# Two transformer blocks in one kernel: first product by blocks of rows, an expert's whole matrix per transfer, attention probabilities scaled after the values

## What is computed

```python
h = rmsnorm(x, attn_norm);  proj = h @ w_in                         # block 1, start
# mixture of experts, per group of 8 experts
hid = silu(einsum('td,edf->tef', h, w_gate[g])) * einsum('td,edf->tef', h, w_up[g]) * combine
y = y + einsum('tef,efd->td', hid, w_down[g])
# block 2, kind 0: window of 128 keys to either side, all context keys, and a sink column
s_loc = where(band_mask, q_a @ k_a.T * scale, -inf);  s_ctx = q_a @ k_ac.T * scale
p = softmax(concat([s_loc, s_ctx, sink]));  o_a = p_loc @ v_a + p_ctx @ v_ac
# block 2, kind 1: neighbourhood of 16 columns, bias rpb, and all context keys
p = softmax(concat([q_b @ k_b.T * scale + bias (masked), q_b @ k_bc.T * scale]))
o_b = p_loc @ v_b + p_ctx @ v_bc
x_new = x + g1 * concat([rms_norm(o_a), rms_norm(o_b)]) @ w_out
```

## Time and profile before

| | us |
|---|---|
| median of three runs | 819.42 |
| lowest, highest | 817.73, 819.96 |
| the profiled execution's own time | 819.99 |
| its span, first to last instruction | 818.2 |
| TensorE busy | 752.5 (92%) |
| mean granted clock of TensorE | 0.986 |

### The profile page before, as it was taken

One profiled execution on the slowest core, in us unless ns is written; L12 is line 12 of the kernel. 1 busy time (PEld: TensorE's weight loads), 2 busy tenths in 40 slices (PEclk: granted clock), 3 DMA queues, 4 the chain that ended last, 5 costly groups with the idle time before them and its releaser, 6 DMA issues. The chain is left out here.

```text
span 818.2 us, 14415 instructions
## 1 busy us (share of the span) xinstructions
PE 752.5 (92%) x5881; PEld 551.5 (67%) x5881; DVE 453.9 (55%) x820; ACT 321.0 (39%) x563; POOL 39.4 (5%) x31
## 2 busy tenths in 40 slices
PE   8999999899998998767868899898999999999998
PEld 5978976554745754543635687656547888888886
DVE  3899755544542233022130796589667766577665
ACT  4667333410442233031240854566542533434431
POOL 1000021010000000000000033100010000000000
PEclk9999999999999999999899999999999999999999
DMA  8894459979899999999999995500008354565201
GB/s 282 288 355 158 152 211 397 333 271 347 327 402 400 407 403 408 402 404 409 403 404 403 401 264 201 205 2 2 1 1 287 137 194 154 185 228 205 103 1 51
DMA packets 130501, 208.40 MB, mean 255 GB/s; under 512 B 7909, under 2 KB 55302, under 8 KB 130318
## 3 DMA queue, kind: packets, MB, share of 16 engines
q1 hardware_dynamic: 129518, 205.39, 68.9%
q10 hardware_dynamic: 864, 2.18, 0.8%
q0 software_dynamic: 64, 0.05, 0.0%
HBM read 206.51 MB, written 1.08 MB: 254 GB/s over the span
## 5 line engine op out<-in xcount | busy, mean ns | idle before, releaser
L2608 DVE TENSOR_TENSOR unit_parts<-ring,unit_parts 128x2048 fp32r<-128x2048 f32 x33 | 75.5, 2289 | 57.2 <-ACT unit_parts L1936 57.2
L1936 ACT ACTIVATE unit_parts<-ring 128x2048 fp32r<-128x2048 f32 x33 | 62.9, 1912 | 73.9 <-PE psa L1313 43.0
L1312 PE MATMUL psv<-column_parts,unit_parts 128*128 128x512 f32 (+1 forms) x192 | 65.5, 389 | 1.6 <-DVE arena L2686 1.4
L1312 PE MATMUL psa<-column_parts,unit_parts 128*128 128x512 f32 (+1 forms) x192 | 65.1, 388 | 0.0
L1020 PE MATMUL psv<-ring,arena 128*32 128x256 f32 x976 | 54.5, 380 | 0.2 <-DMA ring<-in_w_up_dram 0.2
L1313 PE MATMUL psv<-column_parts,unit_parts 128*128 128x256 f32 (+1 forms) x192 | 52.0, 271 | 0.0
L1313 PE MATMUL psa<-column_parts,unit_parts 128*128 128x256 f32 (+1 forms) x192 | 52.0, 271 | 0.0
L2729 POOL TENSOR_TENSOR small<-small,consts 128x2 f32<-128x2 f32 (+4 forms) x15 | 28.2, 1883 | 472.7 <-DVE small L2460 246.2
L954 PE MATMUL psa<-arena 128*128 128x128 f32 x224 | 34.2, 325 | 14.4 <-DMA arena<-in_w_in_dram 14.2
L1020 PEld LDWEIGHTS psv<-ring,arena 128*32 128x32 f32 x976 | 30.8, 110 | 21.0 <-DMA ring<-in_w_up_dram 0.7
L954 PEld LDWEIGHTS psa<-arena 128*128 128x128 f32 x224 | 33.1, 238 | 15.5 <-DMA arena<-in_w_in_dram 15.2
(11 more groups left out here) (436 smaller groups left out, 1726.9 us busy)
## 6 DMA issues: line engine op xcount, KB each, us to landing
ring<-in_w_gate_dram SPq DMA_DIRECT2D x43, 1024.0 KB, 9.5
ring<-in_w_up_dram SPq DMA_DIRECT2D x40, 1024.0 KB, 5.2
arena<-in_w_down_dram SPq DMA_DIRECT2D x32, 1024.0 KB
ring<-in_w_mod_dram SPq DMA_DIRECT2D x24, 1024.0 KB, 7.5
ring<-in_w_in_dram SPq DMA_DIRECT2D x23, 1024.0 KB, 10.9
ring<-in_w_down_dram SPq DMA_DIRECT2D x11, 1024.0 KB, 7.4
ring<-in_w_out_dram SPq DMA_DIRECT2D x8, 1024.0 KB, 8.1
arena<-in_w_in_dram SPq DMA_DIRECT2D x8, 512.0 KB, 12.2
```

The source lines that it names most:

```text
L1312: pe.matmul(both_parts(bank, t_0, t_1), hi, col_parts[:, :, k, t_0:t_1], start=(k == 0), stop=False)
L1936: act.activation(unit_parts[q % 3][:, 0, :], slot_of(NPRE + u_), ACT.Copy).then_inc(upper_done, 1)
L2608: vec.tensor_tensor(lo, slot_of(NPRE + at["mlp"] + 3 * n + kind), hi, ALU.subtract).then_inc(lower_done, 1)
```

## The change

1. **Start.** Scaling, turning and the first product go by blocks of rows: `row_block` (root of one block, `rows_normed` counts each), `turn_block(hn, b)`, `turned_block` in VectorE and ScalarE (four pieces of 128 columns), and `cols_T_first` with 32 matmuls of 128 columns, the second block's turn inside it. GpSimd makes one root per block, so later counts rise by one. SyncE issues four weight units, not two, ahead of the other small vectors.
2. **Experts.** A gate or up unit is one expert's whole matrix, one piece of 8 KB per partition. TensorE waits for all four of a half and then runs over k and the experts. Places are counted free once per half: three counts of `moe_unit_used` a pass.
3. **Attention.** Token keys and context keys lie side by side, so the scores of a tile are one product of 512 columns. For kind 0 VectorE adds the window mask in PSUM (128 x 128) and ends the maxima of two heads in one instruction. Probabilities are turned unscaled, right after the exponential. Once for eight heads the sums are inverted (`shares`), spread over 64 columns per head, turned by four matmuls through a turn bank (`shares_by_query`), copied by ScalarE (`shares_out`), and multiplied into the outputs (`outputs`). Squares are taken of the product. The loops run one turn longer. A small exponential ahead of `heads_out(qbT)` loads its table.
4. The wait at L1096 is split in two, one for each half of k.

The diff, cut to its core:

```diff
             if n < KD:
-                up_half, pair = divmod(n, 4)
-                src = (w_gate, w_up)[up_half][bass.ds(e0, EPG), :, :].rearrange("e (p k) f -> p e (k f)", k=KD)
-                sp.dma_start(v, src[:, :, pair * 2 * FF:(pair + 1) * 2 * FF]).then_inc(expert_landed[n], 32)
+                up_half, e = divmod(n, EPG)
+                src = (w_gate, w_up)[up_half][bass.ds(e0 + e, 1), :, :].rearrange("e (p k) f -> p (e k f)", k=KD)
+                sp.dma_start(mview(n), src).then_inc(expert_landed[n], 32)
...
             pe.wait_ge(rows_normed, 1)
-            turn(hn)
-            pe.wait_ge(v_free, nv)
-            pe.wait_ge(a_free, na)
+            turn_block(hn, 0)
+
+            def cols_T_first():
+
+                bank = PSA[2]
+                w = unit(1)[0]
+                for b in range(NB):
+                    for cc in range(2):
+                        for k in range(KD):
+                            if cc == 0 and k in (0, 4):
+                                pe.wait_ge(*((a_free, 1 + b) if k else (v_free, 2 + b)))
+                            mm = pe.matmul(bank[:, cc * T + b * P:cc * T + b * P + P], w[:, k, cc * P:(cc + 1) * P],
+                                           hT[:, k, b * P:(b + 1) * P], start=(k == 0), stop=(k == KD - 1))
+                        if (b, cc) == (0, 0):
+                            pe.wait_ge(rows_normed, 2)
+                            turn_block(hn, 1)
...
-                    if n in (0, 2):
-                        pe.wait_ge(moe_tokens_copied, 2 * t + 1 + n // 2)
...
+                for up_half in range(2):
+                    for n in range(4 * up_half, 4 * up_half + 4):
+                        if first and n in first_places:
+                            pe.wait_ge(first_landed[n], 32)
+                        else:
+                            pe.wait_ge(expert_landed[n], 32 * t if n in first_places else 32 * t + 32)
                     f0 = up_half * FF
-                    for kk in range(2):
+                    for k in range(KD):
+                        if up_half == 0 and k % 4 == 0:
+                            pe.wait_ge(moe_tokens_copied, 2 * t + 1 + k // 4)
                         for e in range(EPG):
-                            w = first_view(n, e) if first else mview(n)[:, e * 512:e * 512 + 512]
-                            mm = pe.matmul(mG[32 * e:32 * e + 32, f0:f0 + FF], XT[:, 2 * pair + kk, 32 * e:32 * e + 32],
-                                           w[:, kk * FF:(kk + 1) * FF],
-                                           start=(pair == 0 and kk == 0), stop=(pair == 3 and kk == 1))
-                    mm.then_inc(moe_unit_used if n < KD - 1 else moe_gate_up_done, 1)
+                            n = 4 * up_half + e
+                            w = first_view(n, k) if first else mview(n)[:, k * FF:k * FF + FF]
+                            mm = pe.matmul(mG[32 * e:32 * e + 32, f0:f0 + FF], XT[:, k, 32 * e:32 * e + 32], w,
+                                           start=(k == 0), stop=(k == KD - 1))
+                    mm.then_inc(moe_gate_up_done if up_half else moe_unit_used, 1)
...
+                        r0 = HD * (h // 4)
+                        st = [(bank[:], qaT[r0:r0 + HD, h % 4, b * P:(b + 1) * P], keys_a[r0:r0 + HD, 0, :], True, True)]
...
+                        r0 = HD * (h % 2)
+                        st = [(bank[:], qbT[r0:r0 + HD, h // 2, b * P:(b + 1) * P], keys_b[r0:r0 + HD, h // 2, :], True, False)]
+                        for m in range(2):
+
+                            i0, o0 = GRID * (m ^ n % 2), GRID * m
+                            st.append((bank[o0:o0 + GRID, 0:T], c("flip")[i0:i0 + GRID, i0:i0 + GRID],
+                                       bias[b][i0:i0 + GRID, h, :], False, True))
+                    steps.append(st)
...
             def turn2(n):
-                pe.wait_ge(probs2_normed, n + 1)
-                if n >= 2:
-                    pe.wait_ge(probs2_copied, n - 1)
+                pe.wait_ge(exps2_done, n + 1)
...
+            def shares_by_query(k):
+
+                pe.wait_ge(shares_ready, k + 1)
+                t = shares_at(k)
+                pe.wait_ge(probs2_copied, t - 1)
+                for cc in range(4):
+                    mm = pe.matmul(TB[t % 2][:, cc * P:(cc + 1) * P], share_cols[:, 2 * cc:2 * cc + 2, :], ident,
+                                   start=True, stop=True)
                 mm.then_inc(turned2_done, 1)
...
                 if name == "attn":
-                    stream(0, 2)
+                    stream(0, 4)
             sp.dma_start(brow[:], v("b_mod_2").rearrange("l (n c) -> (l n) c", c=P)).then_inc(s_rows, 16)
-            stream(2, 6)
+            stream(4, 6)
...
-                if n == KD - 1:
+                if n in (KD + 1, KD + 3):
+                    sp.wait_ge(moe_down_done, 2 * t - 1 if n == KD + 1 else 2 * t)
+                elif 4 <= n < KD:
                     sp.wait_ge(moe_gate_up_done, t)
-                elif n in (KD + 1, KD + 3):
-                    sp.wait_ge(moe_down_done, 2 * t - 1 if n == KD + 1 else 2 * t)
                 else:
-                    k = n + 1 if n < KD else (8 if n == KD else 9)
-                    sp.wait_ge(moe_unit_used, 9 * t + (k - 9))
+                    sp.wait_ge(moe_unit_used, 3 * t + ({KD: -1, KD + 2: 0}[n] if n >= KD else -2))
...
+            def row_block(b):
+
+                nonlocal nsq
+                nsq += 1
+                dve.wait_ge(squares_done, nsq)
+                rsqrt(ss[:, b:b + 1], rstd[:, b:b + 1], D)
+                vec.tensor_scalar(hn[:, b, :], xres[:, b, :], rstd[:, b:b + 1], None, ALU.mult).then_inc(rows_normed, 1)
+
+            attn = vc[:, ROWS["attn"]:ROWS["attn"] + KD]
+            row_block(0)
             dve.wait_ge(v_free, 1)
-            turned(hT, vc[:, ROWS["attn"]:ROWS["attn"] + KD])
+            row_block(1)
+            for b in range(NB):
+                turned_block(hT, b, attn)
...
-            def norm_probs(n):
-
-                b, kind, h = tiles2[n]
-                j = stat(n)
-                dve.wait_ge(exps2_done, n + 1)
-                total = rs2[:, j:j + 1]
-                if kind == 0:
-                    link(vec.tensor_tensor(total, total, den[:, j:j + 1], ALU.add))
+            def shift_sinks(k):
+
+                dve.wait_ge(max2_done, 8 * k + 8)
+                vec.tensor_tensor(den[:, stats_of(k)], sink[:], nm2[:, stats_of(k)], ALU.add).then_inc(sinks_shifted, 1)
+
+            def shares(k):
+
+                dve.wait_ge(exps2_done, 8 * k + 8)
+                total = rs2[:, stats_of(k)]
+                if k % 2 == 0:
+                    dve.wait_ge(sink_exp_done, k // 2 + 1)
+                    link(vec.tensor_tensor(total, total, den[:, stats_of(k)], ALU.add))
                 link(vec.reciprocal(total, total))
-                vec.tensor_scalar(E2[:, n % 4, :], E2[:, n % 4, :], total, None, ALU.mult).then_inc(probs2_normed, 1)
+                if k >= 1:
+                    dve.wait_ge(turned2_done, shares_at(k - 1) + 1)
+                vec.tensor_copy(share_cols, total.unsqueeze(2).broadcast_to((P, AH, HD))).then_inc(shares_ready, 1)
 
             def outputs(k):
 
                 b, kind = divmod(k, 2)
-                dve.wait_ge(heads_squared, k + 1)
-                vec.tensor_reduce(sqs[:, k, :], sqo[:, k % 2, :, :].rearrange("p c t -> p t c"), AX, ALU.add)
+                dve.wait_ge(values2_done, 8 * k + 8)
+                dve.wait_ge(probs2_copied, shares_at(k) + 1)
+                vec.tensor_tensor(o_scaled, PSX[k % 2][:], share_rows, ALU.mult).then_inc(heads_scaled, 1)
...
+            def max2(p):
+
+                for n in (2 * p, 2 * p + 1):
+                    b, kind, h = tiles2[n]
+                    dve.wait_ge(scores2_done, n + 1)
+                    bank = at["SB"][n % 4]
+                    if kind == 0:
+                        far = bank[:, (1 - b) * P:(2 - b) * P]
+                        link(vec.tensor_tensor(far, far, c("window")[:, b * P:(b + 1) * P], ALU.add))
+                        ins = vec.tensor_reduce(mxt[:, n % 2:n % 2 + 1], bank[:], AX, ALU.max, negate=True)
+                    else:
+                        j = stat(n)
+                        vec.tensor_reduce(nm2[:, j:j + 1], bank[:], AX, ALU.max, negate=True).then_inc(max2_done, 1)
                 if kind == 0:
-                    link(vec.tensor_reduce(mxt[:, n % 2:n % 2 + 1], src, AX, ALU.max))
-                    vec.tensor_scalar(nm2[:, j:j + 1], mxt[:, n % 2:n % 2 + 1], sink[:, h:h + 1], -1.0,
-                                      ALU.max, ALU.mult).then_inc(max2_done, 1)
-                else:
-                    vec.tensor_reduce(nm2[:, j:j + 1], src, AX, ALU.max, negate=True).then_inc(max2_done, 1)
-
-            for p in range(NT // 2 + 3):
+                    link(ins)
+                    j, h0 = stat(2 * p), tiles2[2 * p][2]
```

(2 more changed lines are left out.)

## The result

The changed kernel takes 821.96 us (median of 14 runs, 820.57 to 827.72) against 818.23 for the kernel before (14 runs beside them). The ratio is 1.0043, 95% interval 1.0028 to 1.0058: about 3.5 us slower. The forecast was 815.0 and faster. The time lies inside the range given (811 to 823), on the side that had a chance of 0.23, but it was not that rival's mechanism that took it there, as the experiments show.

A forecast was written before the change was run, and what follows sets the result against it. TensorE, busy 92%, was taken as the bound, with DMA bounding the expert passes. Start −0.6, experts −6.0, attention +2.2 and split wait −0.1 sum to −4.5 us, from 819.42 to 815.0; range 811.0 to 823.0.

The forecast's parts named there:

- A, start: First rows and first product: block-wise turning lets the product end at 19.55 instead of 20.15, −0.6 us (−0.9 to +0.1).
- B, experts: Expert weights: 2.65 us lost to late release, 8.6 gained by longer pieces, together −6.0 us (−8.8 to +2.7).
- C, attention: Second block's attention: savings in scores and start against added turns, stalls and a later norm, +2.2 us (0 to +4.5).
- D, split wait: Wait split in two at L1096: VectorE's next work isn't earlier for it, −0.1 us.
- B, the late release: Expert weights: release by fours delays pass 2's gate issue, 2.65 us lost once; pass 1's 2.05 covered.
- a sign that it is wrong: Expert passes: TensorE's waits for up units appearing in the middle of a pass would show the forecast wrong.
- B, the rate: Expert stream from pass 2: 8 KB pieces save 0.18 us per unit, 48 units, −8.6 us.
- the rival of 421: Expert stream: 8 KB pieces gain only what 4 KB ones do, 421 GB/s; total 819.6 us; chance 0.22.
- The rival without any rise of rate: Expert stream: the rate doesn't rise in a long stream, only the late release is left; 823.5 us; chance 0.23.
- the head start: Second block's attention: first values start at about 528.4, not 531.0, by turning after the exponential and early table load, −2.6 us.
- the three stalls of the shares: Second block's attention: shares pass VectorE, TensorE and ScalarE in row order, waits of 0.7, 2.5 and 0.7, +4.0 us.
- The rival in which the attention stalls less: Second block's attention: shares are turned without waiting, costing 0 instead of +2.2; total 812.7 us; chance 0.12.

The follow-up runs named there:

- e1: Only the start by blocks of rows, with four weight units issued ahead of the small vectors, on the kernel before: 822.15 us, ratio 1.0042.
- e2: Only the whole-matrix expert units and their release by fours, on the kernel before: 815.16 us, ratio 0.9957.
- e3: Only the second block's attention with unscaled probabilities, on the kernel before: 821.97 us, ratio 1.0043.
- e4: The changed kernel with the attention of before (start, experts and split wait kept), against the kernel before: 818.77 us, ratio 0.9998.
- e6: The start by blocks of rows alone, but two weight units ahead of the small vectors as before, against the kernel before: 822.73 us, ratio 1.0047.
- e7: The kernel before with its units and 2 KB pieces kept, but expert waits and release by fours: 820.95 us, ratio 1.0023.

## Why the prediction was wrong, by its own steps

| part | forecast | measured alone | what differed |
|---|---|---|---|
| A, start | −0.6 | +3.5 (e1) | stalls at 126 to 143 us that no step had |
| B, experts | −6.0 | −3.4 (e2) | rate gain mis-sized; late release near its size, lost elsewhere |
| C, attention | +2.2 | +3.4 (e3) | lower clock behind a longer idle time |
| D, split wait | −0.1 | 0 (e4) | 0.7 us gained, waited for again |
| sum | −4.5 | +3.5 | |

The forecast missed by 8.0 us, of which A is 4.1, B 2.6, C 1.2 and D 0.1. The time fell inside the range all the same, near its upper end; that is luck, since the range was drawn there for a rate that doesn't rise, and the rate rose.

**A is the step that failed.** Its working held: the first product ended at 19.5 to 19.6 in e1, e4 and e6, the 19.55 of the sum (18.77 in after), and the two moved units cost nothing (e6). What failed is the silent assumption that 14 more matmuls ahead of 20 us leave the stretch at 130 us alone. Its lower and upper bounds (−0.9 to +0.1) looked at the start only. What the runs showed in its place is +3.5 us, 2.4 of it idle time on "issue" at borders of instruction blocks and about 1 a lower clock behind it. The gain was real (0.2 to 1.3 us at 26 us in the traces) and was lost several times over. Why a block came late is open between the saturated engines and the pace of this stretch.

**B, the late release**, +2.65: the issue is as late as forecast, and the medians show +2.3, but the way there was wrong in both halves. Pass 1, called covered, lost 1.5 us of transfer; pass 2, said to have no backlog, lost 0.4. That the sum came near is partly luck. TensorE's wait for four up units at once was named, with a delay of 1 us within its slack; it waits 7.9 us there in all. The prediction had called such waits a sign that it is wrong. They did appear, but its waits at the line ahead fell (14.2 to 10.0 us at L988), and the stream kept its rate, so the sign didn't mean what it was taken for.

**B, the rate**, was the mis-sized term. 0.18 us per unit came from 8 KB placed between 421 and 449 GB/s. What e2 and e7 show is 5.8/48 = 0.12 per unit, an estimated 425 GB/s for the long pieces, between the forecast and the rival of 421 and nearer to the rival. Measured from issue to issue over four passes, a pass is 32.6 us in e7 and 31.4 in e2, which is 0.15 per unit, so the size is known to some 0.03. The 449 were a window of 3.5 us, with 375 to 385 GB/s in the 4 us ahead of it and 294 in the 2 us behind; a short window picked for its rate is no rate of a long stream. The whole stretch was to show 418 to 425 GB/s and shows 417 in e2 and in after, just below; a pass of 31.5 us was forecast and 31.6 measured. The rival without any rise of rate fell.

**C** was right in its parts: the head start −2.5 (forecast −2.6), the three stalls of the shares 3.9 (4.0), the norm 4.3 us after the last values (4.4). (The sum has 4.0 for three stalls that it lists as 0.7, 2.5 and 0.7, 3.9.) From first to last values it took 4.95 us more where the parts of the sum give +3.1; of the missing 1.85, 1.6 is the clock behind the 2.28 us of idling. In after's trace C is so +4.1 (−2.5, +4.95 and +1.7); the median of e3 says +3.4. The prediction had read the waits and not asked what the clock does behind them. The rival in which the attention stalls less fell.

**D**: against the turn ahead of it, the line behind the split wait starts 0.7 us sooner (2.21 us after that turn's start in after, 2.89 in before), but the product that follows then waits 0.36 us for VectorE and starts 9.72 us after that turn in both, so nothing of it is left.

With A at +3.5, the late release at +2.3, the rate at −5.8, C at +2.2 with 1.6 more for the clock, and D at 0, the same sum gives +3.8, against +3.5 measured. Part of that agreement is by construction, as A, the release and the rate are taken from runs.

## What to carry over

Run the parts of a change alone: here one gain of 3.4 us was hidden by two losses of the same size, and dropping them (with the wide scores kept) turned 0.4% slower into 0.8% faster. A costing that looks only at the stretch that it edits is blind to what lies behind it: compare equal instructions across the whole trace, and where idle time is put down to "issue", look for a packet of the instruction queue that lands just ahead of its end, and pad the stream with a few instructions to see whether it moves. Take a transfer rate from the long stream that resembles the new one, not from the best short window.

## What the runs showed of the hardware

- Seven or fourteen tiny matmuls that delay nothing where they stand make TensorE idle 1.8 and 2.6 us on "issue" over 100 us later, while the DMA engines move 405 GB/s, and cost some 4 us in the end (+3.5 and +4.0 in the medians); with 128 the idle time is gone.
- These idle times stand some 257 recorded TensorE instructions apart and end 1.2 to 1.5 us after a 16 KB packet of the instruction queue has landed.
- A long stream moves 405 GB/s in pieces of 2 KB and 417 with two thirds of it in pieces of 8 KB.
- After 2.28 us of idling TensorE's granted clock was 0.63 and 0.52 over the next 4 us (the lower of its two levels, 1.2 GHz, for most of it), and a group of values took 1.79 us for 1.09. Behind 1.44 us of idling at one place it fell in e4 and did not in before.
- Releasing buffers four at a time made an issue 2.6 us later and cost the stream 1.9 us, 1.5 of them a pass sooner.
- Two executions with the same instructions drifted 1.7 us apart between 110 and 165 us: in that stretch a difference of one trace is no evidence for less than 2 us.
